# A two-block transformer: the second block's attention gets 128-row score products, a later compressed branch, a reciprocal per item and one weight unit less in flight

## The chip, the cores and the metric

The kernel runs on one core of a Trainium2 chip. The metric is the device time of one launch in microseconds, the median of the runs shown. Everything is float32 in and out; most products are made of parts (a value rounded for the fast product, and the rest of it), three products for one.

## The reference, cut to what matters

The program applies two blocks, each of two layers, to 512 tokens of width 1024. The first block is not touched. A layer of the second block:

```python
def hybrid_layer(x, ...):                      # second block, twice
    h = rmsnorm(x, norm_mix)
    q_a, k_a, v_a, f_a, q_b, kv_b, g_b, gate_a, gate_b = split(h @ w_in)
    # Fox: 8 heads of 64, causal softmax(q k / 8 + c_i - c_j) v, c = cumsum(log_sigmoid(f_a + b))
    y_a = from_heads(fox_attention(...)) @ w_o_fox
    # NSA: 8 query heads, 2 key/value heads (4 query heads share one)
    kc, vc, ks, vs, kw, vw = split(kv_b)
    kc, vc = compress_blocks(kc), compress_blocks(vc)   # 31 blocks of 32 tokens -> MLP with GELU
    ks, kw = partial_rope(ks), partial_rope(kw)
    # at 512 tokens the chosen 8 of 8 blocks and the window of 512 are both plain causal attention
    o_c = softmax(q kc / 8, masked to ended blocks) vc
    o_s, o_w = causal(q, ks, vs), causal(q, kw, vw)
    o_n = g0 * o_c + g1 * o_s + g2 * o_w
    y_b = from_heads(o_n) @ w_o_nsa
    x = x + (sigmoid(gate_a) * y_a + sigmoid(gate_b) * y_b) @ w_out
    return x + relu(rmsnorm(x) @ w_up)**2 @ w_down
```

## The kernel before, in words

Each engine has its own program in one file, and all five walk the same plan in the same order; semaphores tie them. `weight_plan` lists the weights as units of at most 128 x 1024 values. SyncE loads unit u into `RAW[u % NRAW]` (L3079), waiting until unit u - NRAW is used up. ScalarE rounds it into `Wh` (L1402, four buffers), VectorE writes the rest in place (`Wl`, L2089), both two units ahead (`AHEAD`). TensorE's main products are L643 to L645, three for each pair of tiles; `lin_s` makes token-major results, `lin_t` channel-major ones, 512 columns each.

What is not a main product runs as a *side*: a generator that advances by one step at each `tick()`, called behind every six main products in most stages (three in the stage `hidden`). All four compute programs hold the same generators, so one step of a side has a part on each engine, and its place among the main work is fixed in each engine's instruction order. `drain` ticks on without main products until a side is done.

`mixing` (L843 TensorE, L1572 ScalarE, L2361 VectorE, `normalise` L3118 GpSimd) is the side for Fox and NSA softmax attention. An item is (block t of 128 queries, group, head). In step i:

- TensorE transposes the normalised weights of item i-3 (`turn`, L858, t+1 products), makes the scores of item i (`head`, L921 and L922, for Fox also L924, and the causal mask L916 in bf16), and multiplies the weights of a finished bundle with the values (`mix`, L879, L880).
- ScalarE copies the turned weights of item i-3 (L1448), then makes the exponentials and their sum of item i (L1582).
- VectorE makes the lower part of the turned weights of i-3 (L2137), inverts sums (L2376), and takes the maximum of the scores of i (L2368).
- GpSimd multiplies the exponentials by the inverted sum (Fox, L3126) or by that and the branch's gate (NSA, L3128).

Items come in bundles of two that share their values: 16 bundles, 32 items for Fox; 32 bundles, 64 items for NSA. A bundle's sums are inverted together, in the step after its second item. NSA takes the query blocks in pairs, (3, 0) first, then (2, 1) (`PAIRS`); an output tile (t, key/value head) takes four bundles, two head pairs in each of the two branches, and is closed by the last. At a closing TensorE first adds the compressed branch (L1299, four products) into the same bank, so every closing waits (`need`, L896) until the side `compressed` is done; the whole side stops there, on all engines.

Scores: the queries stand in 128 partitions, upper part above lower part (for odd or later heads the other way round), the upper key part twice, in both halves. L921 multiplies all 128 rows with it. The lower key part is held once: two heads' (Fox) or two branches' (NSA) parts share one tile, and L922 multiplies 64 rows, the queries' upper part, with it.

The second block's order: values (`fv`), forget gates, keys and queries of Fox group 0, then group 1 with the Fox side beside it, `kc`, `qn`, `ks`, then twice `hidden` (the compression's first matrix) with gates `ga` and output products `oa`, `ga` and `oa` for the rest, `gb`, then `drain(ont)` (L1368), which waits for NSA and the compressed side, then `ob`, `out1` and the feed-forward part. NSA begins in `hidden`; the compressed scores follow the second `hidden`.

Of the kernel before, what the change touches and what calls it, by code (L numbers as in the profile page):

```python
# [34 lines left out]
NRAW = 6  # L35
# [133 lines left out]
class Memory:  # L169


    def __init__(self, nc, ctx):
# [75 lines left out]
        self.QA = [area("QA", [4, S], w, F32R) for w in (5120, 0)]  # L248
        self.KAh = [area("KAh", [4, S], w, F32R) for w in (7168, 2048)]
        self.KAl = [area("KAl", [2, S], w, F32R) for w in (9216, 4096)]  # L250
        self.VF = area("VF", [NT, 8, P], 10240, F32R)
# [4 lines left out]
        self.CR = area("CR", [S], 18432, BF16)  # L256
        self.SEL = area("SEL", [8, P], 18688, BF16)
        self.TQ = area("TQ", [2, S], 19200)

        self.AK = area("AK", [2, 2, S], 6144)  # L260
        self.QNS = area("QNS", [NT, 512], 8192)
        self.VN = area("VN", [NT, 4, P], 4096, F32R)
# [3 lines left out]
        self.QN = area("QN", [8, S], 10240, F32R)  # L266
        self.KSh = area("KSh", [2, 2, S], 6144, F32R)
        self.KSl = area("KSl", [2, S], 8192, F32R)
# [20 lines left out]
        self.CT = [area("CT", [512], w) for w in (22688, 9216)]  # L289
# [329 lines left out]
def tensor_program(pe, M, G, K, plan):  # L619
# [223 lines left out]
    def mixing(B, scores, values, first_mix=None, group=None, extra=None, need=None):  # L843
# [18 lines left out]
        def mix(n):  # L862
# [6 lines left out]
            if B.closes(n) and extra:  # L869
                extra(*items[last], b)  # L870
# [10 lines left out]
            if B.closes(n):  # L881
                x.then_inc(*K.fills(o))
                K.points[tag, n] = K.full(o)
                K.close(o)
            else:
                x.then_inc(*pv.up())
                K.points[tag, n] = pv.now()

        n = len(items)
        for i in range(n + 7):  # L890
# [252 lines left out]
    for l in range(DEPTH):  # L1143
# [15 lines left out]
        def fox_scores(t, g, h, b):  # L1159
            return causal(t, b, M.QA[g][:, h, :], M.KAh[g][:, h, :], M.KAl[g][:, h // 2, :], 64 * (h % 2), (M.SEL[0:96, 4 * g + h, :], M.CR[0:96, :]))  # L1160
# [10 lines left out]
        def fox_side():  # L1171
            yield from idle(FOX_WAIT)
            yield from mixing(fox_bundles(l), fox_scores, lambda t, g, h, k: M.VF[:, k, 4 * g + h, :], fox_values, fox_group)
# [17 lines left out]
        def nsa_scores(t, g, h, b):  # L1191
            return causal(t, b, M.QN[:, h, :], M.KSh[:, g, h // 4, :], M.KSl[:, g, :], 64 * (h // 4))

        def nsa_side():
# [13 lines left out]
            for j in range(4):  # L1208
                pe.wait_ge(*K.drained(f"nq{l} {j}"))
            yield from mixing(nsa_bundles(l), nsa_scores, lambda t, g, h, k: M.VN[:, k, 2 * g + h // 4, :],  # L1210
                              extra=compressed_values, need=("compressed", l))
# [51 lines left out]
        def compressed_side():  # L1263
# [27 lines left out]
            done.add(("compressed", l))  # L1291

        def compressed_values(t, g, h, b):
# [4 lines left out]
            for x in range(4):  # L1298
                pe.matmul(b[0:64, x * P:(x + 1) * P], M.VCB[:, kv, x, :], M.CT[c][:, (2 * s + kv) * P:(2 * s + kv + 1) * P],  # L1299
                          start=False, stop=False, skip_group_check=True)  # L1300
# [81 lines left out]
def scalar_program(sc, M, G, K, plan, a):  # L1382
# [189 lines left out]
    def mixing(B, group=False, take=None, finish=None, need=None):  # L1572
# [20 lines left out]
        for i in range(n + 7):  # L1593
# [4 lines left out]
            if need and c is not None and B.closes(c):  # L1598
# [4 lines left out]
            if i < n:  # L1603
                head(i)
            c = B.ended(i - 6)
# [14 lines left out]
    def packed_q(dst, name, x, gain, r=0):  # L1620
        upper(dst[r:r + 64, :], M.bank[K.of(name)][64 * x:64 * x + 64, :], name, gain)
# [204 lines left out]
    for l in range(DEPTH):  # L1826
# [19 lines left out]
        def fox_q(c):  # L1846
            def evac(j, name):
                sc.wait_ge(*K.drained(name))
                for x in range(2):
                    r = slice(64 * x, 64 * x + 64)  # L1850
                    sc.activation(M.QA[c][r, 2 * j + x, :], M.TQ[r, j, :], ACT.Copy).then_inc(*hi.up())
# [54 lines left out]
        def heads_side(j):  # L1906
            yield
            if j < 4:
                for x in range(2):
                    packed_q(M.QN[:, 2 * j + x, :], f"nq{l} {j}", x, 0.125, 64 * (j // 2))  # L1910
# [6 lines left out]
        def nsa_side():  # L1917
# [10 lines left out]
            yield from mixing(nsa_bundles(l), take=nsa_take, need=("compressed", l))  # L1928
# [29 lines left out]
        def compressed_side():  # L1958
# [14 lines left out]
            done.add(("compressed", l))  # L1973

# [10 lines left out]
        def on_side():  # L1985
            while nsa in sides.open or compressed in sides.open:
                yield
            for j in range(4):
                for t in range(NT):
                    sc.wait_ge(*K.drained(f"{tag} o{t}{j // 2}"))  # L1990
# [18 lines left out]
        def fox_v(s, name):  # L2009
            if s == 0:  # L2010
                sc.wait_ge(G.rstd, n + 1)
            upper(M.VF[:, s, :, 0:64], M.bank[K.of(name)][:, :].rearrange("p (h d) -> p h d", d=64), name, M.r(n, s))
# [56 lines left out]
def vector_program(ve, M, G, K, plan):  # L2069
# [291 lines left out]
    def mixing(B, group=False, add_up=None, finish=None, need=None):  # L2361
# [22 lines left out]
        for i in range(n + 7):  # L2384
# [4 lines left out]
            if need and c is not None and B.closes(c):  # L2389
# [4 lines left out]
            c = B.ended(i - 1)  # L2394
            if c is not None:
                invert(c)
            if i < n:
                head(i)
            c = B.ended(i - 6)
# [14 lines left out]
    def packed_q(dst, name, x, gain, r=0):  # L2414
        return lower(dst[64 - r:128 - r, :], M.bank[K.of(name)][64 * x:64 * x + 64, :], dst[r:r + 64, :], gain)
# [315 lines left out]
    for l in range(DEPTH):  # L2731
# [45 lines left out]
        def fox_q(c):  # L2777
            def evac(j, name):
                ve.wait_ge(G.fox_lo, fox_lo.n - 1)
                by_token(M.TQ[:, j, :], name, n, 0.125)  # L2780
                for x in range(2):
                    q, r = M.QA[c][:, 2 * j + x, :], 64 * x
# [416 lines left out]
```

## Time and profile before

| | |
|---|---|
| median of 3 runs | 3051.8 us (3051.73 to 3054.97) |
| profiled execution, time | 3052.99 us |
| its span | 3051.2 us |
| TensorE busy | 2855.3 us, 94% |
| VectorE busy | 1476.4 us, 48% |
| ScalarE busy | 1225.5 us, 40% |
| GpSimd busy | 163.2 us, 5% |
| mean granted TensorE clock | 0.965 |
| weights read | 226 MB on SyncE's queue, 76 GB/s over the span |

The second block's first layer begins near 1200 us and its attention stage ends near 1700 us; the second layer repeats it some 920 us later. "PE" is TensorE's products, "PEld" its weight loads, "DVE" VectorE, "ACT" ScalarE, "POOL" GpSimd. Busy times of TensorE are lengths of pipelined products; starts tell more than lengths.

### The profile page before, as it was taken

The page shows a single profiled execution, that of the slowest core. Times are in us where ns is not written, and L with a number is a line of the kernel's source. Part 1 is how long each engine was busy: PE and PEld are TensorE (multiplying, and loading weights), DVE is VectorE, ACT ScalarE, POOL GpSimd, SP SyncE. Part 2 cuts the span into 40 slices and gives each one's busy share as a digit, 9 for nine tenths or more (in the row PEclk, how much of TensorE's full clock was granted, in tenths as well). Part 3 has the DMA queues.
Part 4 walks back from the last instruction along what each step waited for, and adds up shares of the span by engine and source line. Part 5 has one row for each costly group of instructions (what it writes and reads, how often), then busy time and mean ns, then how long its engine had stood idle before and what let it go on. Part 6 is the DMA issues. An engine that isn't in the chain of part 4 may idle for free. (4 is left out here: it accounts for less than half of the span.)

```text
span 3051.2 us, 34802 instructions
## 1 busy us (share of the span) xinstructions
PE 2855.3 (94%) x13625; PEld 2309.7 (76%) x13625; DVE 1476.4 (48%) x2551; ACT 1225.5 (40%) x2166; POOL 163.2 (5%) x221
## 2 busy tenths in 40 slices
PE   7999999998899999889898999999889888999998
PEld 6777888886788888667666788888667666788886
DVE  6754343466543434546444543344546444553343
ACT  4543222364432223445455432233445455342231
POOL 1000000000000000030112000000030112000000
PEclk9899999999999999999998999999999998899999
DMA  4113333220133332213210233333213210233332
GB/s 130 35 36 90 97 97 97 88 83 19 56 95 96 99 97 87 62 35 101 61 47 28 64 95 97 97 97 87 69 35 97 63 49 28 61 98 97 97 97 69
DMA packets 186357, 231.40 MB, mean 76 GB/s; under 512 B 11874, under 2 KB 140356, under 8 KB 186196
## 3 DMA queue, kind: packets, MB, share of 16 engines
q1 hardware_dynamic: 184500, 225.95, 24.5%
q0 software_dynamic: 976, 1.32, 0.3%
q8 instruction: 109, 1.79, 0.2%
q10 hardware_dynamic: 720, 1.92, 0.2%
q14 instruction: 52, 0.43, 0.0%
HBM read 227.05 MB, written 2.11 MB: 75 GB/s over the span
## 5 line engine op out<-in xcount | busy, mean ns | idle before, releaser
L2089 DVE TENSOR_TENSOR Wl<-RAW,Wh 128x1024 fp32r<-128x1024 f32 (+3 forms) x434 | 511.5, 1200 | 401.7 <-ACT Wh L1402 401.0
L1402 ACT ACTIVATE Wh<-RAW 128x1024 fp32r<-128x1024 f32 (+3 forms) x434 | 438.0, 1032 | 369.4 <-PE bank L645 368.9
L643 PE MATMUL bank<-Hh,Wh 128*128 128x512 f32 (+1 forms) x976 | 394.3, 404 | 5.9 <-DVE Wl L2089 4.3
L645 PE MATMUL bank<-Hh,Wl 128*128 128x512 f32 (+1 forms) x976 | 385.3, 395 | 0.0
L644 PE MATMUL bank<-Hl,Wh 128*128 128x512 f32 (+1 forms) x976 | 384.9, 394 | 0.0
L643 PE MATMUL bank<-Wh,A 128*128 128x512 f32 x864 | 337.2, 390 | 0.0
L645 PE MATMUL bank<-Wh,A 128*128 128x512 f32 x864 | 336.3, 389 | 0.0
L644 PE MATMUL bank<-Wl,A 128*128 128x512 f32 x864 | 336.1, 389 | 0.0
L643 PE MATMUL bank<-HA,Wh 128*128 128x512 f32 x704 | 276.7, 393 | 7.2 <-DVE HA L2138 7.2
L645 PE MATMUL bank<-HA,Wl 128*128 128x512 f32 x704 | 275.5, 391 | 0.0
L644 PE MATMUL bank<-HA,Wh 128*128 128x512 f32 x704 | 275.3, 391 | 0.0
L643 PEld LDWEIGHTS bank<-Hh,Wh 128*128 128x128 f32 (+1 forms) x976 | 184.9, 189 | 45.4 <-DVE Wl L2089 5.1
L645 PEld LDWEIGHTS bank<-Hh,Wl 128*128 128x128 f32 (+1 forms) x976 | 184.3, 189 | 41.6
L644 PEld LDWEIGHTS bank<-Hl,Wh 128*128 128x128 f32 (+1 forms) x976 | 184.6, 189 | 34.7
L643 PE MATMUL bank<-Wh,Hh 128*128 128x512 f32 (+2 forms) x512 | 206.7, 404 | 4.1 <-DVE Wl L2089 2.7
L2137 DVE TENSOR_TENSOR PT<-bank,PT 128x384 fp32r<-128x384 f32 (+1 forms) x192 | 94.3, 491 | 229.6 <-ACT PT L1448 228.7
L645 PE MATMUL bank<-Wh,Hl 128*128 128x512 f32 (+2 forms) x512 | 195.0, 381 | 0.0
L644 PE MATMUL bank<-Wl,Hh 128*128 128x512 f32 (+2 forms) x512 | 194.2, 379 | 0.0
L645 PEld LDWEIGHTS bank<-Wh,A 128*128 128x128 f32 x864 | 162.2, 188 | 33.8
L644 PEld LDWEIGHTS bank<-Wl,A 128*128 128x128 f32 x864 | 162.2, 188 | 33.2
L643 PEld LDWEIGHTS bank<-Wh,A 128*128 128x128 f32 x864 | 162.2, 188 | 33.2
L858 PE MATMUL bank<-CST,P 128*128 128x128 f32 x480 | 99.2, 311 | 89.8 <-POOL P L3128 54.9
(371 smaller groups left out, 4489.8 us busy)
## 6 DMA issues: line engine op xcount, KB each, us to landing
RAW<-in_w_up_dram SPq DMA_DIRECT2D x108, 512.0 KB, 3.7
RAW<-in_w_down_dram SPq DMA_DIRECT2D x108, 512.0 KB, 3.7
RAW<-in_w_in_dram SPq DMA_DIRECT2D x90, 512.0 KB, 3.6
RAW<-in_w_gate_dram SPq DMA_DIRECT2D x44, 512.0 KB, 3.7
RAW<-in_w_out_dram SPq DMA_DIRECT2D x28, 512.0 KB, 3.7
RAW<-in_cmp_w_dram SPq DMA_DIRECT2D x16, 512.0 KB, 3.9
RAW<-in_w_o_fox_dram SPq DMA_DIRECT2D x8, 512.0 KB, 4.0
RAW<-in_w_o_nsa_dram SPq DMA_DIRECT2D x8, 512.0 KB, 3.4
```

The lines of the kernel that those rows point to most:

```text
L643: pe.matmul(o, sh, mh, start=first, stop=False)
L644: pe.matmul(o, sh, ml, start=False, stop=False)
L645: return pe.matmul(o, sl, mh, start=False, stop=last)
L858: x = pe.transpose(b[:, k * P:(k + 1) * P], e[:, k * P:(k + 1) * P], ident)
L1402: sc.activation(M.Wh[:, v % NHL, 0:n], M.RAW[:, v % NRAW, 0:n], ACT.Copy).then_inc(G.w_hi, 1)
L2089: ve.tensor_tensor(M.Wl[:, v % NRAW, 0:n], M.RAW[:, v % NRAW, 0:n], M.Wh[:, v % NHL, 0:n].bitcast(F32), ALU.subtract).then_inc(G.w_lo, 1)
L2137: return ve.tensor_tensor(lo, src, h.bitcast(F32), ALU.subtract)
```

## The change

- `NRAW` goes from 6 to 5. The freed 4 KB per partition move the second block's tiles: lower key parts get twice the room, the values of Fox are two tiles of four heads.
- Queries always stand upper part above lower part; the lower key part is written to both halves of 128 partitions for each head or branch; L922 takes 128 rows. It adds the product of the two lower parts.
- The wait for the compressed branch stands before the closings of blocks 2 and 1 alone. For blocks 3 and 0 the compressed branch's four products go into a bank of their own (`cv`) once the compressed side is done, and VectorE adds that bank to the output.
- Each item's sum is inverted by itself, in the step after the item, and GpSimd waits per item. Fox's normalising takes a second factor, one.
- NSA's `mixing` has 6 steps after its last item in place of 7.

```diff
-NRAW = 6
+NRAW = 5
@@ Memory
-        self.KAl = [area("KAl", [2, S], w, F32R) for w in (9216, 4096)]
-        self.VF = area("VF", [NT, 8, P], 10240, F32R)
+        self.KAl = [area("KAl", [4, S], w, F32R) for w in (10240, 4096)]
+        self.VF = [area("VF", [NT, 4, P], w, F32R) for w in (12288, 18432)]
-        self.KSl = area("KSl", [2, S], 8192, F32R)
+        self.KSl = area("KSl", [2, 2, S], 10240, F32R)
-        self.CT = [area("CT", [512], w) for w in (22688, 9216)]
+        self.CT = [area("CT", [512], w) for w in (22688, 23944)]
...
@@ TensorE
-            if B.closes(n) and extra:
+            if extra and B.closes(n) and items[last][0] in PAIRS[1]:
                 extra(*items[last], b)
...
             c = B.ended(i - 5)
-            if need and c is not None and B.closes(c):
+            if need and c is not None and B.closes(c) and items[i - 5][0] in PAIRS[1]:
                 while need not in done:
                     yield
...
-    def causal(t, b, q, kh, kl, r, extra=None):
-
+    def causal(t, b, q, kh, kl, extra=None):
         w = (t + 1) * P
         pe.matmul(b[:, 0:w], q[:, t * P:w], kh[:, 0:w], start=True, stop=False)
-        pe.matmul(b[:, 0:w], q[r:r + 64, t * P:w], kl[r:r + 64, 0:w], start=False, stop=extra is None)
+        pe.matmul(b[:, 0:w], q[:, t * P:w], kl[:, 0:w], start=False, stop=extra is None)
...
             done.add(("compressed", l))
-
-        def compressed_values(t, g, h, b):
+            for t in PAIRS[0]:
+                for kv in range(2):
+                    while f"{tag} o{t}{kv}" not in done:
+                        yield
+                    b = fresh(f"cv{l} {t}{kv}")
+                    compressed_values(t, 1, 4 * kv, b, True).then_inc(*K.fills(f"cv{l} {t}{kv}"))
+                    yield
+                    K.close(f"cv{l} {t}{kv}")
+                    yield
...
@@ VectorE
-        def invert(n):
-
-            i = B.ends[n] - 1
-            (t0, _, h0), (t1, _, h1) = B.bundles[n]
-            sums, fac = (M.STT[:, x, t0:t1 + 1, h0:h1 + 1] for x in (1, 4))
+        def invert(i):
+            t, g, h = items[i]
             ve.wait_ge(*K.drained(f"{tag} s{i}"))
-            ve.reciprocal(fac, sums).then_inc(*rec.up())
+            ve.reciprocal(M.STT[:, 4, t, h:h + 1], M.STT[:, 1, t, h:h + 1]).then_inc(*rec.up())
...
-            c = B.ended(i - 1)
-            if c is not None:
-                invert(c)
+            if 0 <= i - 1 < n:
+                invert(i - 1)
             if i < n:
                 head(i)
...
                 for x in range(2):
-                    r = slice(64 * x, 64 * x + 64)
-                    i = lower(M.KAl[c][r, j, :], M.TQ[r, j, :], M.KAh[c][r, 2 * j + x, :])
+                    ve.wait_ge(*hi.due())
+                    for r in (0, 64):
+                        i = ve.tensor_tensor(M.KAl[c][r:r + 64, 2 * j + x, :], M.TQ[64 * x:64 * x + 64, j, :],
+                                             M.KAh[c][r:r + 64, 2 * j + x, :].bitcast(F32), ALU.subtract)
                 i.then_inc(*fox_lo.up())
...
+            for t in PAIRS[0]:
+                for kv in range(2):
...
+                    name = f"cv{l} {t}{kv}"
+                    b = M.bank[K.of(name)][:, :].rearrange("p (j x c) -> p j x c", x=2, c=P)
+                    ve.wait_ge(*K.full(name))
+                    ve.wait_ge(*K.drained(f"{tag} o{t}{kv}"))
+                    for x in range(2):
+                        y = M.ONS[64 * x:64 * x + 64, 2 * kv:2 * kv + 2, t * P:(t + 1) * P]
+                        i = ve.tensor_tensor(y, y, b[0:64, :, x, :], ALU.add)
+                    i.then_inc(*K.empties(name))
+                    yield
...
@@ GpSimd
         for i, (t, g, h) in enumerate(B.items):
-            if B.place[i][1] == 0:
-                gp.wait_ge(*rec.due())
+            gp.wait_ge(*rec.due())
             e = B.exps(M, i)
-            fac = M.STT[:, 4, t, h:h + 1]
...
+            gp.tensor_scalar(e, e, M.STT[:, 4, t, h:h + 1], gate(t, g, h), ALU.mult, ALU.mult).then_inc(G.norm, 1)
...
-        normalise(fox_bundles(l), lambda t, g, h: None)
+        normalise(fox_bundles(l), lambda t, g, h: M.ONE[:, 0:1])
```

## Rows read from the trace of the kernel before

**Rows 1.** Windows: stretch, length, busy us (instructions) by engine, PE clock, DMA share, GB/s.

```profile
1262.00:1383.00 121.00, 97.40 (x482) 71.41 (x483) 59.84 (x115) 58.86 (x132) 34.37 (x30) 0.93 0.12 35
1440.00:1492.00 52.00, 43.07 (x206) 32.06 (x206) 23.99 (x56) 28.45 (x63) 9.60 (x16) 0.87 0.17 50
1492.00:1548.00 56.00, 52.32 (x274) 43.39 (x274) 26.40 (x43) 20.26 (x27) 0.00 (x0) 1.00 0.27 75
1548.00:1643.00 95.00, 83.89 (x436) 62.26 (x434) 43.63 (x96) 62.60 (x124) 17.43 (x29) 0.98 0.15 45
1643.00:1700.00 57.00, 47.90 (x203) 34.14 (x204) 24.97 (x60) 25.03 (x70) 11.42 (x20) 0.67 0.00 1
```

**Rows 2.** Waits of TensorE, whole run: who for whom, us, times, longest.

```profile
PE bank L858 <- POOL P L3128: 54.9, 47, 4.1
PE bank L858 <- POOL P L3126: 30.0, 16, 9.5
...
PE bank L643 <- DVE Wl L2089: 7.0, 3, 2.7
```

**Rows 3.** Groups of GpSimd by shape: count, busy us, mean ns, idle before.

```profile
L3126 POOL TENSOR_SCALAR P<-P,STT 128x512 f32<-128x512 f32 x16 | 27.8, 1740 | 0.0
L3128 POOL TENSOR_SCALAR P<-P,STT,GS 128x512 f32<-128x512 f32 x32 | 24.4, 771 | 289.4 <-DVE STT L2376 289.4
```

**Rows 4.** Waits, 1548 to 1643 us.

```profile
ACT P L1582 <- DVE STT L2368: 22.9, 21, 1.7
ACT PT L1448 <- PE bank L858: 14.5, 9, 7.8
...
PE bank L858 <- POOL P L3128: 9.3, 9, 1.6
```

**Rows 5.** Timeline of TensorE, where the next main stage begins.

```profile
1696.41 0.47 PE L643 MATMUL bank<-ONh,Wh 128*128 128x512 f32 x1 [2.56 <-DVE ONl L2137]
1696.72 0.39 PE L644 MATMUL bank<-ONl,Wh 128*128 128x512 f32 x1
1696.95 0.39 PE L645 MATMUL bank<-ONh,Wl 128*128 128x512 f32 x1
```

**Rows 6.** Timeline of TensorE near 1600 us, an NSA score of 256 columns.

```profile
1600.31 0.36 PE L921 MATMUL bank<-KSh,QN 128*128 128x256 f32 x1
1600.60 0.38 PE L922 MATMUL bank<-KSl,QN 64*128 64x256 f32 x1
1600.91 0.23 PE L916 MATMUL bank<-CMB,IDB 128*128 128x128 bf16 x1
```

**Rows 7.** Timeline of TensorE near 202 us, a score of the first block.

```profile
202.57 0.36 PE L1089 MATMUL bank<-KH,QP 128*128 128x256 f32 x1
202.77 0.28 PE L1090 MATMUL bank<-KL,QP 128*128 128x256 f32 x1
202.89 0.55 PE L803 MATMUL bank<-V,TMP 128*128 128x64 f32 x4
```

**Rows 8.** Groups of ScalarE, 1548 to 1643 us: count, busy, mean ns, idle before.

```profile
L1582 ACT ACT_TABLE_LOAD x8 | 10.3, 1283 | 0.1
```

**Rows 9.** Groups of VectorE, 1200 to 1720 us.

```profile
L2376 DVE RECIPROCAL STT<-STT 128x2 f32<-128x2 f32 x48 | 7.5, 157 | 0.9 <-ACT P L1582 0.9
L2845 DVE TENSOR_TENSOR ONS<-ONS,bank 64x256 f32<-64x256 f32 x16 | 6.8, 423 | 10.8 <-ACT ONS L1891 10.7
...
L2137 DVE TENSOR_TENSOR KAl<-TQ,KAh 64x512 fp32r<-64x512 f32 x8 | 5.5, 686 | 7.8 <-ACT KAh L1859 7.8
```

**Rows 10.** Waits, 1262 to 1383 us.

```profile
ACT PT L1448 <- PE bank L858: 15.6, 16, 2.6
```

**Rows 11.** Waits, 1440 to 1492 us.

```profile
ACT PT L1448 <- PE bank L858: 6.1, 3, 2.2
```

**Rows 12.** Page, parts 5 and 6: weight loads; transfers, us to landing.

```profile
L645 PEld LDWEIGHTS bank<-Hh,Wl 128*128 128x128 f32 (+1 forms) x976 | 184.3, 189 | 41.6
...
RAW<-in_w_in_dram SPq DMA_DIRECT2D x90, 512.0 KB, 3.6
```

More of the change, by code:

```diff
@@ L841, in attend, with mixing @@
             yield
-    def mixing(B, scores, values, first_mix=None, group=None, extra=None, need=None):
+    def mixing(B, scores, values, first_mix=None, group=None, extra=None, need=None, tail=7):
         tag, items = B.tag, B.items
@@ L884, in mix @@
                 K.close(o)
+                done.add(o)
             else:
@@ L889, in mixing @@
         n = len(items)
-        for i in range(n + 7):
+        for i in range(n + tail):
             if group and i < n and (i == 0 or items[i][1] != items[i - 1][1]):
@@ L1210, in nsa_side @@
             yield from mixing(nsa_bundles(l), nsa_scores, lambda t, g, h, k: M.VN[:, k, 2 * g + h // 4, :],
-                              extra=compressed_values, need=("compressed", l))
+                              extra=compressed_values, need=("compressed", l), tail=6)
         def hidden(kv):
@@ L1570, in attend, with mixing @@
             yield
-    def mixing(B, group=False, take=None, finish=None, need=None):
+    def mixing(B, group=False, take=None, finish=None, need=None, tail=7):
         tag, items = B.tag, B.items
@@ L1592, in mixing @@
         n = len(items)
-        for i in range(n + 7):
+        for i in range(n + tail):
             if group and i < n and (i == 0 or items[i][1] != items[i - 1][1]):
@@ L1597, in mixing @@
             c = B.ended(i - 5)
-            if need and c is not None and B.closes(c):
+            if need and c is not None and B.closes(c) and items[i - 5][0] in PAIRS[1]:
                 while need not in done:
@@ L1604, in mixing @@
                 head(i)
+            if c is not None and B.closes(c):
+                done.add(B.outs[c])
             c = B.ended(i - 6)
@@ L1927, in nsa_side @@
             yield from idle(5)
-            yield from mixing(nsa_bundles(l), take=nsa_take, need=("compressed", l))
+            yield from mixing(nsa_bundles(l), take=nsa_take, need=("compressed", l), tail=6)
         def hidden(kv):
@@ L2011, in fox_v @@
                 sc.wait_ge(G.rstd, n + 1)
-            upper(M.VF[:, s, :, 0:64], M.bank[K.of(name)][:, :].rearrange("p (h d) -> p h d", d=64), name, M.r(n, s))
+            b = M.bank[K.of(name)][:, :].rearrange("p (h d) -> p h d", d=64)
+            sc.wait_ge(*K.full(name))
+            for g in range(2):
+                i = sc.activation(M.VF[g][:, s, :, 0:64], b[:, 4 * g:4 * g + 4, :], ACT.Copy, scale=M.r(n, s))
+            i.then_inc(*hi.up())
         def nsa_kv(s, name):
@@ L2359, in attend, with mixing @@
             yield
-    def mixing(B, group=False, add_up=None, finish=None, need=None):
+    def mixing(B, group=False, add_up=None, finish=None, need=None, tail=7):
         tag, items = B.tag, B.items
@@ L2383, in mixing @@
         n = len(items)
-        for i in range(n + 7):
+        for i in range(n + tail):
             if group and i < n and (i == 0 or items[i][1] != items[i - 1][1]):
@@ L2388, in mixing @@
             c = B.ended(i - 5)
-            if need and c is not None and B.closes(c):
+            if need and c is not None and B.closes(c) and items[i - 5][0] in PAIRS[1]:
                 while need not in done:
@@ L2393, in mixing @@
                 turn(i - 3)
-            c = B.ended(i - 1)
-            if c is not None:
-                invert(c)
+            if 0 <= i - 1 < n:
+                invert(i - 1)
             if i < n:
                 head(i)
+            if c is not None and B.closes(c):
+                done.add(B.outs[c])
             c = B.ended(i - 6)
@@ L2412, in main_part, with packed_q @@
         return begin(side)
-    def packed_q(dst, name, x, gain, r=0):
-        return lower(dst[64 - r:128 - r, :], M.bank[K.of(name)][64 * x:64 * x + 64, :], dst[r:r + 64, :], gain)
+    def packed_q(dst, name, x, gain):
+        return lower(dst[64:128, :], M.bank[K.of(name)][64 * x:64 * x + 64, :], dst[0:64, :], gain)
     def packed_k(pairs, name):
@@ L2898, in nsa_side @@
             yield from idle(5)
-            yield from mixing(nsa_bundles(l), add_up=nsa_sum, need=("compressed", l))
+            yield from mixing(nsa_bundles(l), add_up=nsa_sum, need=("compressed", l), tail=6)
         def hidden(kv):
@@ L2979, in compressed_side @@
             done.add(("compressed", l))
+            for t in PAIRS[0]:
+                for kv in range(2):
+                    while f"{tag} o{t}{kv}" not in done:
+                        yield
+                    yield
+                    name = f"cv{l} {t}{kv}"
[6 more added lines that the diff above has]
+                    i.then_inc(*K.empties(name))
+                    yield
         def values_side():
```

71 lines of the change are left out of this document (35 added, 36 removed).

## The prediction

> **What bounds the kernel now.** I read the busy shares by stretch first, to find where TensorE is not full. In the feed-forward stages it has no gap, so the change can earn nothing there. In the second block's attention stage it has gaps [rows 1]: of the 381 us of the five stretches (first layer; the second repeats it) TensorE is busy 97.4 + 43.1 + 52.3 + 83.9 + 47.9 = 324.6, so 56 us are idle, and the clock there is 0.93, 0.87, 1.00, 0.98 and 0.67. The sum of (1 - clock) x length is 36 us. The names below: a *tick* is one step of the softmax side, one (block of queries, head) item, normally laid behind six main products.
>
> Second, who TensorE waits for: 54.9 + 30.0 us of 3051 stand before the transposes of the weights (L858), released by GpSimd's normalising [rows 2]. Third, who that one waits for. GpSimd's two items of a bundle hang on one reciprocal (no idle time before the second item's 16 [rows 3]), which VectorE issues one tick after the *second* item. The nine waits between 1548 and 1643 us, 1.6 us at most [rows 4], all stand before a bundle's first item.
>
> Fourth, what is behind it. ScalarE and VectorE hand each other every item: copy of the turned weights (ACT) -> its lower part (DVE) -> maximum (DVE) -> exponential (ACT) -> next copy. In the stretch 1548 to 1643 ScalarE waits 22.9 us for VectorE's maximum and only 14.5 us for TensorE [rows 4]. The busy times of the two add to 106.2 us in 95 us [rows 1]: a ring with little overlap. The reader should see this beside the TensorE waits: when TensorE gets faster, this ring is next.
>
> Fifth, the order of work. From 1492 to 1548 us no item runs (POOL x0 in [rows 1]), since the first closing of an output waits for the compressed branch. The items missed there run at the end: from 1643 us on no main product is left, the DMA share is 0.00 and the clock 0.67 [rows 1], until the next stage's first one at 1696.4 us, which itself waits 2.56 [rows 5]. In ticks: 18 before the stop; 192 main products, so 32 ticks, during it; 29 with main products after; 24 without.
>
> **Part 1, score products with 128 rows.** At 256 columns the first product starts at 1600.31, the 64-row one 0.29 later, the next instruction 0.31 later [rows 6]. Main 512-column products follow each other by 0.23 [rows 5], so the 0.31 is not streaming. The first block has the same pair with 128 rows in both: 0.20 and 0.12 [rows 7]. Saving (0.29 + 0.31) - (0.20 + 0.12) = 0.28 us an item, 192 items, 54 us of TensorE work. Ends: 0 (if the gap comes from the bf16 mask product that follows, which the first block's pair lacks) and 0.28; I take 0.28, the like pair. It is worth its price only where TensorE sets the tick.
>
> A rule speaks against this step. The Trainium skill, "TensorE: Matmul & The Clock Gate", Part 3, The mechanism, says that a weight load overlaps running products only when it goes to another row group; by it the 64-row load would be the hidden one and the 128-row load not. The trace disagrees as far as it goes: the 64-row product follows late and the 128-row pairs follow at 0.12 [rows 6, 7]. "TensorEngine Tiling (Array Packing)", Key Properties, has the opposite sign: changing the tiling mode drains the array. That fits both gaps.
>
> **Part 2, the waiting point moves.** Only outputs of the second pair of query blocks (2, 1) still wait for the compressed branch. Their first closing is item 45, reached at tick 50, and the stop was at tick 18 for 32 ticks: the two meet, so the stop goes nearly whole. The softmax has 70 ticks now (tail 6): 18 + 32 + 20, and the last 9 of the main ticks run without items. The 24 bare ticks vanish, and with them the low clock and that wait of 2.56.
>
> Time of a tick, if the ring bounds it: 95 us for 29 ticks is 3.28. Of ScalarE's 14.5 us of waiting for TensorE one wait of 7.8 began before the stretch; 6.7 are real [rows 4]. (95 - 6.7) / 29 = 3.04 us. In the former stop sigmoids now alternate with exponentials, and each change loads a table, 1.28 us [rows 8]; I take six more loads, about half of each hidden: 0.1 a tick, so 3.15. TensorE's own need is 83.9 / 29 - 0.28 = 2.6, so it is not the bound.
> From 1492.0: 32 x 3.15 + 20 x 3.04 + 9 x 1.45 (six main products at 0.23, and what slips in) + 2 for what follows = 177 us against 204.4 now (to 1696.4). Saved: 27.5.
>
> The compressed part of blocks 3 and 0 now comes by itself: the same 16 products, a bank for a tick, and eight additions on VectorE of 0.42 [rows 9], 3.4 us in the ring, of which 2 are the term just used (the others fall in the nine bare main ticks). Nobody but the last split waits for them.
>
> **Part 3, a reciprocal per item.** The first item of a bundle is normalised one tick earlier, 2.4 us or more, and the waits in question are at most 1.6 us [rows 4], so they go. Late next is the ring. Cost: 48 more reciprocals of 0.16 [rows 9], 7.5 us a layer, in the ring's half that VectorE holds; 0 if it waits for ScalarE's copy there anyway, so I take half. In the Fox stretch: 121 us, less ScalarE's 15.6 us of waiting for TensorE [rows 10], is 105.4; plus half of 16 x 0.16 (1.3), plus four lower key parts at 0.69 [rows 9] (next part) 2.7: 109.4. The first wait, 9.5 us [rows 2], is the ring filling behind the key evictions and stays for the most part, so I take 112: saved 9 (2 to 12). The NSA reciprocals' half, 32 x 0.16 / 2 = 2.6, is within the rounding of the tick (0.04 each) and left in the range. First 18 NSA ticks: 6.1 us of ScalarE waiting for TensorE [rows 11]; I take 4 of it (0 to 6).
>
> **Part 4, what is held twice.** Lower key parts: Fox 8 more VectorE instructions a layer, NSA 4 more, 0.69 each [rows 9]. Half of the Fox ones precede the first score, where TensorE's main products already stand for VectorE's weight parts; 2.7 us, with the NSA ones partly hidden in the idle ticks ahead of that stage: -3 us a layer (0 to -8). The value tile in two halves splits 8 evictions, under 0.2 each beside 4 x 5 us of products: nothing. GpSimd's multiply by one is a gain: with two factors 512 columns take it 0.77 us, with one 1.74 [rows 3]. The form is about half as long at every width, so Fox items are ready 0.3 to 1.0 us sooner. That lies beside the ring; I count 1 us a layer, for the first wait (0 to 5).
>
> **Part 5, five units in flight.** SP's wait for unit u-6 becomes u-5. A transfer lands in 3.6 us [rows 12]; the weights of unit u are first touched when unit u-4 is done, one unit (24 x 0.23 = 5.5 us) after the issue, and TensorE needs them three units later. All TensorE's waits for weight parts are 7.0 us in the whole run [rows 2]. Cost 0 (0 to 10 if the short hidden units of 12 products run dry).
>
> **Sum.** A layer: 27.5 + 9 + 4 - 3 + 1 = 38.5; two layers 77 us. The profiled execution took 3053.0 (span 3051.2); 3053 - 77 = 2976, and against the median of 3051.8, 2975 us.
>
> **Rivals.**
> *A, TensorE sets the tick.* For it: it is busy 324.6 of the 381 us, and the waits of [rows 2] are its own. Then the idle 56, the clock's 36 and the products' 27 us a layer go, less some 25 for what stays (first Fox wait, compressed steps, bank waits): 95 a layer, 2862 us. Against it: the ring's 106 us in 95.
> *B, the ring overlaps a little worse* with compressed work and Gelu tables in it: T = 3.3, 52 x 3.3 + 15 = 187, saved 17; with 5 for Fox, 2 and -3: 21 a layer, 3010 us.
> *C, the ring eats it all (slower).* If ScalarE and VectorE overlap nowhere in the 52 ticks, each costs the sum of both, 3.66 (106.2 / 29), and 0.14 for hand-overs: 3.8. 52 x 3.8 + 15 = 213, 8.6 over 204.4; the Fox part then gains nothing and pays its 4.0 of new instructions, and the -3 stays: 15.6 a layer, 3084 us. It decides from T = 3.5 on ((204.4 - 15 - 7) / 52). Against: the same mix ran at 3.28.
> *D, the products gain nothing.* If the gap belongs to the bf16 product, TensorE needs 2.9 a tick, just under the ring: some 5 us less gained a layer, 2985. If a 128-row load (0.19, [rows 12]) stood bare in each item besides, it would need 3.08, equal to the ring: some 8 us less gained a layer, 2991. That second case is what the skill's rule on row groups would give here.
> *E, the stop stays* because the compressed branch is not ready at tick 50. Nine ticks of delay cost nothing, the nine main ticks at the end take them. Each further one makes a stopped tick (56 / 32 = 1.75) and a bare one ((1696.4 - 1643) / 24 = 2.2) out of one mixed at 3.15: 0.8 us. At worst 23 x 0.8 = 18 a layer, 3011 us.
>
> **Chances.** Forecast 0.50 and D 0.05 (2950 to 3003); between it and A, and A, 0.20; B 0.12 and E at its worst 0.05 (3003 to 3035); C 0.05; no change 0.03. The likeliest one's own range is 2950 to 3003; for 8 in 10 I take 2900 to 3020. Faster by over 0.2% (6 us, about what a measurement here can tell from none): 0.92; within: 0.03; slower: 0.05.
>
> **What would show it.** The gap after the second score product falls from 0.31 to 0.12 (256 columns) and no L858 wait is left before a bundle's first item. NSA items run without a stop, the next main stage follows the last gate product at once, no stretch of DMA share 0. The Fox part lasts 112 us, NSA ticks 3.0 to 3.2, ScalarE + VectorE busy over 1.15 of those stretches, TensorE still with gaps. The forecast is wrong if ticks come at 2.6 (A) or 3.5 and more (C), or if waits for RAW transfers appear.

## The result and the profile after

The changed kernel takes 2973.55 us (median of 4 runs, 2973.51 to 2974.36); the kernel before took 3052.7 on the same chip (4 runs). The ratio is 0.974, 95% interval 0.9723 to 0.9757. The forecast was 2975. The profiled execution has a span of 2972.6 us, with a mean granted TensorE clock of 0.973 (before: 0.965), TensorE busy for 2786.2 us (94%, 69 less than before), GpSimd for 131.9 (31 less).

The same stages by stretch, first layer of the second block: Fox; the first 18 NSA items; the 32 items that now run where the side stood still; the last 14 items; the tail up to the next main stage. Columns: stretch, length, busy us (instructions) of TensorE's products, its loads, VectorE, ScalarE and GpSimd, granted clock, DMA share, GB/s. They answer to [rows 1].

```profile
1264.00:1371.00 107.00, 85.53 (x464) 67.67 (x463) 59.84 (x130) 55.19 (x126) 18.17 (x30) 0.92 0.13 40
1431.00:1480.00 49.00, 39.23 (x216) 31.34 (x217) 26.83 (x70) 28.65 (x63) 9.90 (x17) 0.90 0.16 50
1480.00:1590.00 110.00, 93.08 (x534) 74.99 (x533) 58.03 (x146) 59.64 (x134) 20.05 (x33) 0.95 0.13 39
1590.00:1634.00 44.00, 41.18 (x246) 33.24 (x245) 23.22 (x59) 30.73 (x60) 7.99 (x13) 1.00 0.16 48
1634.00:1659.00 25.00, 23.24 (x114) 18.47 (x113) 13.34 (x23) 11.38 (x21) 1.11 (x2) 1.00 0.20 65
```

The stretch without items is gone (GpSimd has 33 instructions in the third line), and so is the end without weights to read, where the granted clock was 0.67: the last two lines have clock 1.00 and DMA shares of 0.16 and 0.20. The first product of the next main stage (input `ONh`) follows the last gate product at 0.23 us, as in any main stage, and waits for nothing; before it stood 2.56 idle [rows 5]:

```profile
1658.24 0.39 PE L645 MATMUL bank<-Hh,Wl 128*128 128x512 f32 x1
1658.47 0.39 PE L643 MATMUL bank<-ONh,Wh 128*128 128x512 f32 x1
```

It comes at 1658.5 in place of 1696.4, and in the second layer the last product on `ONh` of this line comes at 2560.4 in place of 2639.0: 37.9 us in the first layer and 40.7 in the second, 78.6 together.

TensorE's own account of that time, from the first Fox score to the first product on `ONh`, both layers, before and then after (columns as above):

```profile
1262.60:1696.41 433.81, 374.69 (x1863) 284.75 (x1864) 218.56 (x431) 226.88 (x461) 74.33 (x96) 0.92 0.17 50
2181.86:2617.86 436.00, 374.11 (x1864) 284.08 (x1864) 218.55 (x431) 226.86 (x461) 74.19 (x96) 0.92 0.17 50
```

```profile
1264.69:1658.47 393.78, 337.94 (x1865) 271.74 (x1863) 226.91 (x496) 221.02 (x457) 58.59 (x96) 0.95 0.18 54
2145.92:2539.35 393.43, 339.01 (x1864) 271.80 (x1863) 226.93 (x496) 221.25 (x457) 58.60 (x96) 0.94 0.18 54
```

The two stages are 83 us shorter. TensorE is busy for 72 us less in them and idle for only 11 us less (121 before, 110 now). Of the 72, some 47 are the shorter score pairs, as experiment 1 will show. The other 25 go with the granted clock, which rose from 0.92 to 0.94 and 0.95: an estimate from these rows, (749 x 0.92 - 47) / 0.945, gives 679 us of busy time where 677 stand. This is how the time divides, and not yet what caused it.

A score of 256 columns, against [rows 6]:

```profile
1604.88 0.36 PE L921 MATMUL bank<-KSh,QN 128*128 128x256 f32 x1
1605.08 0.28 PE L922 MATMUL bank<-KSl,QN 128*128 128x256 f32 x1
1605.20 0.23 PE L917 MATMUL bank<-CMB,IDB 128*128 128x128 bf16 x1
```

0.20 and 0.12, where 0.29 and 0.31 stood. 512 columns gain as much (0.41 + 0.43 went to 0.31 + 0.24), 128 columns a little less (0.24 + 0.26 to 0.15 + 0.11). The bf16 product still follows, so the second gap belonged to the 64 rows.

TensorE's waits in the whole run (who for whom: us, times, longest), against [rows 2], and the waits from 1480 to 1590 us, against [rows 4]:

```profile
PE bank L858 <- POOL P L3157: 43.6, 24, 7.3
PE bank L1285 <- DVE CB L2986: 10.5, 4, 3.3
PE bank L643 <- DVE Wl L2110: 10.2, 3, 3.8
```

```profile
ACT P L1592 <- DVE STT L2389: 37.7, 29, 2.7
DVE PT L2158 <- ACT PT L1458: 25.8, 17, 5.3
...
ACT PT L1458 <- PE bank L858: 10.0, 6, 4.3
```

The 63 waits for GpSimd (84.9 us) are now 24 (43.6). Not all of that is won: other waits in the same place grew, 4.6 us more for `OAy` and 8.8 that are new, for `ONS`, both written by VectorE. In the second fence both halves of the ring are seen: ScalarE waits for VectorE's maximum (L2389), VectorE for ScalarE's copy (L1458). GpSimd's groups by shape (count, busy, mean ns), against [rows 3]:

```profile
L3157 POOL TENSOR_SCALAR P<-P,STT,GS 128x512 f32<-128x512 f32 x32 | 24.7, 771 | 169.2 <-DVE STT L2394 169.2
...
L3157 POOL TENSOR_SCALAR P<-P,STT,ONE 128x512 f32<-128x512 f32 x16 | 12.4, 773 | 62.7 <-DVE STT L2394 62.7
```

### The profile page after: what moved, and what is told of

Its sections match the earlier page's. It is cut to its first block, busy times and chain, and to the rows that moved or that the text cites. A ratio compares the mean times of both kernels' runs of the same rounds, so it can differ in the third digit from the quotient of the medians.

```text
span 2972.6 us, 34957 instructions
## 1 busy us (share of the span) xinstructions
PE 2786.2 (94%) x13625; PEld 2286.9 (77%) x13625; DVE 1497.9 (50%) x2695; ACT 1215.4 (41%) x2169; POOL 131.9 (4%) x221
## 4 chain that ended last, share of the span: by engine, by line
PE 74%; DVE 13%; ACT 7%; issue 4%; DMA 0%; POOL 0%; ACTq 0%; DVEq 0%; SPq 0%; POOLq 0%
PE bank L643 22%; PE bank L645 22%; PE bank L644 22%; DVE Wl L2110 2%; ACT Wh L1412 2%; DVE PT L2158 2%; DVE STT L2389 1%; PE bank L803 1%; ACT P L1592 1%; ACT PT L1458 1%; PE bank L858 1%; PE bank L879 1%; PE bank L740 1%; DVE KAl L2814 1%; PE bank L1103 1%
## 5 line engine op out<-in xcount | busy, mean ns | idle before, releaser
L1592 ACT ACTIVATE P<-bank,STT 128x384 f32<-128x384 f32 (+1 forms) x192 | 101.4, 528 | 219.5 <-DVE STT L2389 219.3
L644 PEld LDWEIGHTS bank<-Wl,A 128*128 128x128 f32 x864 | 162.2, 188 | 33.3
L643 PEld LDWEIGHTS bank<-Wh,A 128*128 128x128 f32 x864 | 162.2, 188 | 33.3
L2158 DVE TENSOR_TENSOR PT<-bank,PT 128x384 fp32r<-128x384 f32 (+1 forms) x192 | 93.9, 489 | 169.2 <-ACT PT L1458 168.4
```

The costliest lines, as they stand in the source:

```text
L643: pe.matmul(o, sh, mh, start=first, stop=False)
L644: pe.matmul(o, sh, ml, start=False, stop=False)
L1592: sc.activation(e, M.bank[K.of(name)][:, 0:e.shape[1]], ACT.Exp, bias=M.STT[:, 0, t, h:h + 1], accum_out=M.STT[:, 1, t, h:h + 1]).then_inc ...
L2158: return ve.tensor_tensor(lo, src, h.bitcast(F32), ALU.subtract)
```

## The experiments

The kernel before was timed beside each set; its median was 3053.99 us in the set of the first four, 3052.5 in the second four and 3054.4 in the last four. A price is given against the changed kernel (2973.55) or against the seventh one (2933.46). Between sets the scale moves by up to 2 us, so 9 to 12, which are compared across two sets, are uncertain by that much beside their own spread.

**1. The second score product takes 64 rows again.** Everything else stays, the keys held twice too.

```diff
-        pe.matmul(b[:, 0:w], q[:, t * P:w], kl[:, 0:w], start=False, stop=extra is None)
+        pe.matmul(b[:, 0:w], q[0:64, t * P:w], kl[0:64, 0:w], start=False, stop=extra is None)
```

> The changed kernel with the second score product on 64 rows again (queries' upper part times one copy of the lower key part); every other edit stays, the second copies are still written. Ring theory (ScalarE and VectorE hand each item back and forth and set the tick; TensorE has spare time in it): TensorE gets the 0.28 us an item back, 54 us in all, but most of it lies in its gaps: 2978 to 2995 us. TensorE theory (its work sets the tick): all 54 us come back, 3027 us. In both the gap from the second product to the mask goes from 0.12 to 0.31 us at 256 columns.

2995.82 us (2995.44 to 2996.95), 0.981 (0.9796 to 0.9825): 22 us more. The gaps are back in the timeline:

```profile
1598.85 0.36 PE L921 MATMUL bank<-KSh,QN 128*128 128x256 f32 x1
1599.15 0.38 PE L922 MATMUL bank<-KSl,QN 64*128 64x256 f32 x1
1599.46 0.23 PE L917 MATMUL bank<-CMB,IDB 128*128 128x128 bf16 x1
```

TensorE's busy time grows by 47 us (2833.5), and 22 us reach the end: two fifths of the 54, just over the range that the ring theory gave and far from the other's 3027. The rest lies in what had been idle time of TensorE: its span less its busy time falls from 186 to 161 us, 12 of them in the waits for GpSimd in front of the transposes (43.6 to 31.3). The step pays, less than its own length.

**2. All closings wait for the compressed branch again.**

```diff
-            if need and c is not None and B.closes(c) and items[i - 5][0] in PAIRS[1]:
+            if need and c is not None and B.closes(c):
...
-            for t in PAIRS[0]:
+            for t in ():
```

> The changed kernel with every closing waiting for the compressed branch again, its four products added at each closing, no separate bank and no later addition; the rest stays. My terms: part 2 without what the shorter tick gives is some 20 us a layer, so 3014 us; 32 ticks without items come back and 23 bare ones with DMA share 0 behind the last main product. Rival (the stop only moves work, the ring has the same items to do either way): 2974 to 2985 us.

3009.09 us (3008.75 to 3010.62), 0.9854 (0.9839 to 0.9869): 35.5 us more, for my 40. Stop and bare end are back, in two lines of the windows (columns as above):

```profile
1480.00:1536.00 56.00, 52.32 (x276) 43.51 (x275) 26.96 (x45) 20.95 (x28) 0.77 (x1) 1.00 0.26 75
1632.00:1675.00 43.00, 29.13 (x164) 23.36 (x164) 19.54 (x59) 19.84 (x59) 9.79 (x16) 0.81 0.00 0
```

In the second, TensorE is busy 29 of 43 us; what it lacks is paid there, with the 2.57 before the next main stage. The granted clock of the whole run falls with it, from 0.973 to 0.968. The moved waiting point is the largest single part of the change.

**3. One reciprocal for a bundle again.**

```diff
-            if 0 <= i - 1 < n:
-                invert(i - 1)
+            if B.ended(i - 1) is not None:
+                invert(B.ended(i - 1))
...
-            gp.wait_ge(*rec.due())
+            if B.place[i][1] == 0:
+                gp.wait_ge(*rec.due())
```

> The changed kernel with one reciprocal per bundle of two items again, issued one tick after the second item, and GpSimd waiting once per bundle; the rest stays. If the wait of a bundle's first item was a bound of its own, its waits before the transposes come back and the time is 2995 to 3015 us. If the ring alone sets the tick, the earlier reciprocal earns nothing, and without it VectorE has 96 instructions of 0.16 us less: 2968 to 2976 us.

2998.04 us (2993.90 to 3001.23), 0.9816 (0.9802 to 0.9831): 24 us more, though VectorE has 96 instructions less. Who waits, in the whole run:

```profile
PE bank L858 <- POOL P L3160: 100.1, 50, 11.0
```

Against 43.6 in the changed kernel and 84.9 in the one before: with the other parts of the change in place the late reciprocal is waited for longer. TensorE's busy time is 3 us less than in the changed kernel, so all that it costs is waiting.

**4. The kernel before with five weight units in flight.**

```diff
-NRAW = 6
+NRAW = 5
```

> The kernel before with NRAW = 5 and nothing else. My term for one weight unit less in flight: 0, so within 0.1% of the kernel before (3050 to 3055 us), no wait for a weight transfer. Rival: the short units in the stage hidden run dry and it costs up to 10 us.

3054.99 us, 1.0002 (0.9992 to 1.0012): nothing, as forecast.

**5. Every maximum of `mixing` twice.** The second result is the one used.

```diff
-            ve.tensor_reduce(M.STT[:, 0, t, h:h + 1], ..., AX.X, ALU.max, negate=True).then_inc(*mx.up())
+            for x in (2, 0):
+                r = ve.tensor_reduce(M.STT[:, x, t, h:h + 1], ..., AX.X, ALU.max, negate=True)
+            r.then_inc(*mx.up())
```

> The changed kernel with VectorE's maximum of each item taken twice (the first one into an unused column), some 0.45 us more in the ScalarE-VectorE ring for each of 192 items, 87 us in all; TensorE's work is untouched. The 64-row run gave 22 of 54 us back, so TensorE sets the tick in about two fifths of it and the ring in the rest. Ring theory: 3015 to 3045 us. TensorE theory (VectorE is half idle and hides it): below 2985 us.

3038.11 us (3036.07 to 3040.21), 0.9955 (0.9938 to 0.9971): 64 us more. The group of maxima grew by 76 us (90.8 to 167.1, less than the 87 of the expectation), so 0.84 of each added microsecond of VectorE is seen at the end, although VectorE is busy for only half of the span. Not all of it is waiting. The same two stages as in the section on the result:

```profile
1266.33:1689.97 423.64, 350.42 (x1864) 279.32 (x1863) 264.99 (x592) 219.76 (x457) 58.53 (x96) 0.92 0.17 50
2177.43:2601.03 423.60, 351.94 (x1864) 279.92 (x1863) 264.91 (x592) 219.70 (x457) 58.53 (x96) 0.92 0.17 50
```

They are 60 us longer than in the changed kernel. TensorE is idle for 35 us more and busy for 25 us more, though it has no product more: the granted clock was 0.92 where it had been 0.94 and 0.95. The waiting alone is thus under half of the 76 us; no run holds the clock still to part the two.

**6. No product with the lower key part in `mixing`.** The computation lacks that term.

```diff
-        pe.matmul(b[:, 0:w], q[:, t * P:w], kh[:, 0:w], start=True, stop=False)
-        pe.matmul(b[:, 0:w], q[:, t * P:w], kl[:, 0:w], start=False, stop=extra is None)
+        pe.matmul(b[:, 0:w], q[:, t * P:w], kh[:, 0:w], start=True, stop=extra is None)
```

> The changed kernel without the product with the lower key part (scores of the second block lack that term; its parts are still written). It takes 0.12 to 0.24 us of TensorE work out of each item, some 31 us in all, and nothing from ScalarE or VectorE. Ring with two fifths TensorE: 2958 to 2966 us. TensorE theory: 2943 us. Ring alone: 2970 to 2974 us.

2969.98 us (2967.60 to 2970.80), 0.9728 (0.9714 to 0.9743): 4 us less (3 to 6 over its runs), of 31 us of work taken from TensorE. In the two stages TensorE is idle for 16 us more, and its busy time falls by 23 and not by 31: the granted clock fell too, to 0.93 and 0.94. With 5 this weighs the two engines: of VectorE's time 0.84 counts, of TensorE's 0.12, the clock's answer included in both. Between 64 and 128 rows it was still 0.41, so TensorE's weight drops as its work gets less.

**7. The order in VectorE alone.** In a step VectorE takes the maximum first and the lower part of the turned weights last. No instruction is added or removed.

```diff
-            if 0 <= i - 3 < n:
-                turn(i - 3)
+            if i < n:
+                head(i)
             if 0 <= i - 1 < n:
                 invert(i - 1)
-            if i < n:
-                head(i)
+            if 0 <= i - 3 < n:
+                turn(i - 3)
```

> The changed kernel with VectorE's order in a step turned round: maximum of item i first, then the reciprocal of i-1, then the lower part of the turned weights of i-3. All the same instructions. The maximum then no longer stands behind ScalarE's copy, which breaks the ring: the two engines work beside each other. Ring theory: 2900 to 2950 us, TensorE's gaps in these stages mostly gone. If the ring was not the bound: 2970 to 2980 us, and if the later lower part holds up values or banks, slower than that.

2933.46 us (2933.43 to 2935.80), 0.9612 (0.9597 to 0.9626): 40 us less than the changed kernel, and faster than both. The timeline of a Fox step in the changed kernel (start, us, engine, line, operation, in brackets the idle time before it and who ended it):

```profile
1341.42 0.28 ACT L1458 ACTIVATE PT<-bank 128x128 fp32r<-128x128 f32 x1
1341.73 0.29 DVE L2158 TENSOR_TENSOR PT<-bank,PT 128x128 fp32r<-128x128 f32 x1 [1.02 <-ACT PT L1458]
1341.94 0.15 DVE L2394 RECIPROCAL STT<-STT 128x1 f32<-128x1 f32 x1
1342.12 0.69 DVE L2389 TENSOR_REDUCE STT<-bank 128x1 f32<-128x512 f32 x1
...
1342.85 0.69 ACT L1592 ACTIVATE P<-bank,STT 128x512 f32<-128x512 f32 x1 [1.15 <-DVE STT L2389]
```

VectorE idles 1.02 for the copy, ScalarE then 1.15 for the maximum: one works, the other stands. With the order turned round:

```profile
1340.02 0.69 DVE L2389 TENSOR_REDUCE STT<-bank 128x1 f32<-128x512 f32 x1 [1.52 <-PE bank L917]
1340.63 0.15 DVE L2394 RECIPROCAL STT<-STT 128x1 f32<-128x1 f32 x1
1340.70 0.27 DVE L2158 TENSOR_TENSOR PT<-bank,PT 128x128 fp32r<-128x128 f32 x1
1340.75 0.69 ACT L1592 ACTIVATE P<-bank,STT 128x512 f32<-128x512 f32 x1 [1.15 <-DVE STT L2389]
```

The lower part now lies beside the exponential and waits for nothing. In the whole run VectorE's waits for ScalarE's copy fall from 168.4 to 25.6 us and ScalarE's for the maximum from 219.3 to 122.8; here it is still 1.15, since the maximum itself now starts after a wait. What VectorE waits for instead is TensorE's scores, and ScalarE waits longer for TensorE's transposes (49.0 us before this edit, 99.0 with it). The group of maxima of the whole run, first the changed kernel, then this one (idle before them at the end of the line):

```profile
L2389 DVE TENSOR_REDUCE STT<-bank 128x1 f32<-128x384 f32 (+1 forms) x192 | 90.8, 473 | 0.3
```

```profile
L2389 DVE TENSOR_REDUCE STT<-bank 128x1 f32<-128x384 f32 (+1 forms) x192 | 93.5, 488 | 107.9 <-PE bank L917 106.3
```

**8. Fox normalised with one factor**, as in the kernel before.

```diff
-            gp.tensor_scalar(e, e, M.STT[:, 4, t, h:h + 1], gate(t, g, h), ALU.mult, ALU.mult).then_inc(G.norm, 1)
+            fac = M.STT[:, 4, t, h:h + 1]
+            if gate(t, g, h) is None:
+                gp.tensor_scalar(e, e, fac, None, ALU.mult).then_inc(G.norm, 1)
...
```

> The changed kernel with GpSimd's Fox normalising by one factor again, 0.60 to 1.74 us in place of the two-factor form's 0.45 to 0.77. Forecast: the first wait and a few others of the Fox stage lengthen, 2974 to 2985 us, mine is 2977. If GpSimd stood on the path of every Fox item, 64 x 0.5 = 32 us come back: 3005 us.

2975.87 us (2974.01 to 2976.08), 0.9747 (0.9733 to 0.9762): 2 us, at the edge of what can be told. GpSimd's times doubled at 512 columns for it:

```profile
L3159 POOL TENSOR_SCALAR P<-P,STT 128x512 f32<-128x512 f32 x16 | 25.1, 1566 | 53.6 <-DVE STT L2394 53.6
```

**9. Order of 7, 64 rows of 1.** The two edits together.

> The turned-round order of VectorE (maximum first, 2933.5 us) with the second score product back at 64 rows, which costs TensorE 0.28 us an item, 54 us in all. In the order of the changed kernel that cost 22 us. If the ring between ScalarE and VectorE was what hid the rest there, it hides less here: 2963 to 2987 us, likeliest 2975. If the products' price does not depend on the ring (it falls into other waits): 2955 us, again 22.

2957.20 us (2955.29 to 2960.22), 0.9685 (0.9669 to 0.9701): 24 us over the seventh. My 2975 was wrong, the rival's 2955 right: what the products cost does not depend on the order in VectorE. The ring had not been what hid the other 30 us. The pages show where they went: TensorE is busy for 39 us more and idle for 19 us less than in experiment 7.

**10. The kernel before with that order alone.**

```diff
-            if 0 <= i - 3 < n:
-                turn(i - 3)
+            if i < n:
+                head(i)
             c = B.ended(i - 1)
...
-            if i < n:
-                head(i)
+            if 0 <= i - 3 < n:
+                turn(i - 3)
```

> The kernel before with only VectorE's order in a step of mixing turned round (maximum, then the bundle's reciprocal, then the lower part of the turned weights); the stop, the bundle's reciprocal and the 64-row product stay. If the ring set the ticks outside the stop already: 3.28 us a tick falls to TensorE's own 2.9 for some 29 ticks a layer (11 us), the 24 bare ticks by 0.3 or more (7), Fox by 5: 23 us a layer at most, so 3000 to 3035 us, likeliest 3020. If the wait for the bundle's reciprocal set the pace of the old kernel, the order is worth little: 3045 to 3055 us.

3013.15 us (3010.25 to 3017.52), 0.9866 (0.9852 to 0.9881): 41 us less than before, half of what the whole change brought. In the first layer 21.6 us, 15.8 of them from the first score behind the stop on. Waits of TensorE:

```profile
PE bank L858 <- POOL P L3128: 32.1, 26, 3.9
PE bank L858 <- POOL P L3126: 26.8, 12, 9.7
```

Of the 84.9 us of [rows 2], 58.9 are left: part of what stood under GpSimd's name was the order in VectorE.

**11. Order of 7, maxima twice as in 5.**

> The turned-round order with every maximum of mixing taken twice (the second result is the one used), 87 us of VectorE work in all. In the changed kernel's order that cost 64 us. If the new order halves the ring (a hand-over from copy to copy now takes two steps in place of one), VectorE has room: 10 to 35 us over 2933.5, so 2943 to 2968. If VectorE's work sits on the path whatever the order: 64 us again, 2997.

2985.35 us (2975.22 to 2987.50), 0.9768 (0.9750 to 0.9786): 52 us over the seventh, between my 10 to 35 and the rival's 64, nearer to the rival. Of 76 us 0.68 still counts, by its fastest run 0.55. As in 5 TensorE, with no product more, is busy for longer, 24 us in the whole run, at a granted clock of 0.968 against 0.977.

**12. Order of 7, no lower key part's product, as in 6.**

> The turned-round order without the lower key part's score product (left out of the computation), 31 us of TensorE work in all. In the changed kernel's order leaving it out gained 4 us. If TensorE sets the ticks once the order is turned round: 15 to 31 us gained, 2902 to 2918 us. If the ring still sets them: 2926 to 2931.

2924.33 us (2919.45 to 2928.54), 0.9574 (0.9560 to 0.9588): 9 us less than the seventh (5 to 14 over its runs), again between the two (15 to 31, or 2 to 7). The new order did not hand the bound over to TensorE alone.

## Why the prediction was right, step by step

The time is right (2975 forecast, 2973.55 measured), and the waiting point, the reciprocal, the keys and the five units did what the prediction said of them. The sum is partly luck: sizes inside the terms were off and cancelled, the score products, which were to earn nothing beside the ring, carried 22 us that were booked under other names, and the granted clock, priced as a term only in rival A, rose over both stages as a whole. First layer, starts of scores in both traces, cut at the same main product:

| | forecast, us | measured, us |
|---|---|---|
| waiting point moved, and tail, from the 18th NSA score | 27.5 | 24.3 (205.0 to 180.7) |
| Fox, with GpSimd's two factors | 9 + 1 | 10.5 (117.1 to 106.7) |
| NSA, first to 18th score | 4 | 5.9 (51.8 to 45.9) |
| keys held twice | -3 | -2.7 (first Fox score 2.1 later, 0.6 more before NSA) |
| a layer | 38.5 | 37.9; second layer 40.7 |
| two layers | 77 | 78.6 |

**The waiting point.** Right, also in its place: before NSA item 50 the trace shows 12 main products in place of 6, so the side stops for one tick. It had stopped for 33 and not 32: four ticks of that stretch lie in `hidden`, where a tick follows three main products. My sum took no stopped tick. The ticks there were mis-sized: 109.8 us, less 1.75 for the stopped one, is 3.38 for each of 32, where I took 3.15. I had struck all of ScalarE's waiting for TensorE from the tick; 10.0 us of it stand in the waits from 1480 to 1590, 0.3 a tick. The 0.1 for more table loads was wrong too: from the 18th NSA item to the end of the stage there are 19 loads, and there were 21. In these 32 steps the tick was rival B's (3.3), behind them it was not.

The last 14 items came at 3.03 (forecast 3.04). The six steps of the tail and eight bare main ticks took 26.4, for which I had 6 x 3.04 + 9 x 1.45 + 2 = 33.3: a tail step has no score, maximum or exponential, and I priced it as a full one. 32 x 0.23 + 1.75 = 9.1 is too little and 33.3 - 26.4 = 6.9 too much. The stretch that I compared with (204.4) also began before the 18th item's own tick was over, and my sum has no tick for it: 2.1 more. That is 180.7 measured from the 18th score against 177 forecast, by errors that for the most part cancel.

**The products.** The saving of 0.28 us holds at 256 columns (0.29 at 512, 0.24 at 128). The prediction gave it no term of its own, since the ring was to set the tick; experiment 1 shows that it carries 22 of the 79 us. So the Fox, NSA and tail terms, which I had put down to waits and to the ring, contained it. In a loop of engines that wait for each other in turn, "not the bound" is not "free". The Trainium skill, "TensorEngine Tiling (Array Packing)", Key Properties, has the sign right: a change of tiling mode drains the array, and experiment 1 puts 0.28 us on the two changes around one 64-row product. The rule of the Trainium skill in "TensorE: Matmul & The Clock Gate", Part 3, The mechanism, by which a 128-row load behind a 128-row product would stand bare (rival D's second case), is not what the trace shows: 128 rows behind 128 rows follow at 0.11 to 0.31. The prediction also read too much into that rule: the 64 rows are among the 128 that the products around them use, so by it the 64-row load would not have been the hidden one either.

**A reciprocal per item.** Right: 24 us by experiment 3. The forecast that all waits of L858 for GpSimd go was too strong, 43.6 us in 24 remain. Two of 7.3 are the start of the Fox side, which I had let stand; the other 22 make 29 us.

**GpSimd, keys held twice, five units.** GpSimd's second factor: 2 us for two layers (forecast 2), though the time is not halved at every width as I had it; at 128 columns it goes from 0.60 to 0.45. Keys: about 5 (forecast 6; by the starts in the table, no experiment). Five units: 0 (forecast 0, experiment 4).

**What was to be seen.** Besides the waits of L858, two of the signs failed: NSA ticks were to come at 3.0 to 3.2 (3.38, then 3.03), and the busy times of ScalarE and VectorE were to add to over 1.15 of the stretches; they are (59.84 + 55.19) / 107 = 1.08 for Fox, 1.07 in the 32 steps and 1.23 only behind them. A sum near 1 is what strict turns give, so a lower one meant more of a ring, and I had the sign of this test wrong.

**The parts against the whole.** Undone one at a time they cost 22 + 35.5 + 24 + 2 = 83.5 us; less some 5 for the keys, 78.5. The whole is 79, so the parts add, to within the 2 us by which the sets differ.

**The rivals.** A (TensorE sets the tick) is out: taking 31 us from TensorE gained 4, and TensorE's idle time in the two stages fell only from 121 to 110 us. What A had and my sum had not is the clock: (1 - clock) x length of the two stages fell by some 26 us. C is out: the tick was 3.38 at worst, and C decides from 3.5 on. D is out by the gaps, 0.12 with the bf16 product still behind them. E took the one tick.

**The ring.** Shown: VectorE's time counts for 0.84, TensorE's for 0.12 in the changed kernel, with what the clock adds or takes, and the order alone is worth 40 us in both kernels; in the changed one TensorE's idle time gives 31 of 39 us of the two stages. Not right is my picture of it as the single bound that the new order halves: experiments 9, 11 and 12 all missed by it. TensorE's scores, then the maximum, then the exponential, then the next copy still follow each other, with TensorE inside the loop (106.3 us of VectorE's waiting). That this loop is what keeps 0.68 of a maximum on the path is argued from these waits; no run took the loop apart, and none parted its waiting from the slower clock, so it stays open.

## What to carry to other kernels

Where two engines share a step, look for a consumer placed ahead of a producer on the same engine: here the order of three lines, with no work changed, was worth half of what the whole change brought. Price a part of a loop of engines by adding or removing a known amount of its work on each engine, and not by busy shares: VectorE was 50% busy, and 0.84 of what was added to it counted. Look at the granted clock of such a run beside its time: here waiting elsewhere also made TensorE's own products longer. A waiting point in a side task moves work: the stop itself looks harmless, and the missed work is paid for where it then runs bare.

## What the runs showed of the hardware that was not expected

- A 64-row product between 128-row ones costs 0.09 to 0.10 us before it and 0.14 to 0.20 behind it, at 128 to 512 columns.
- GpSimd's tensor_scalar over 128x512 takes 0.77 us with two factors and 1.57 to 1.74 with one; at 128 columns 0.45 and 0.60.
